# Second-layer loads on another queue, gathered rows ahead of weights, a last sum behind a branch, and one projection by groups of banks, in a two-layer hybrid trunk

## The reference

```python
for i in range(2):
    xn = rms_norm(h, norm_mix[i])
    pa, pb, pc, pg = split(xn @ w_in[i])
    ya = stick_breaking_attention(pa)              # branch A
    yb = rwkv7_time_mix(pb, xn, v_first, ...)      # branch B, a recurrence over time
    yc = swa_sink_attention(pc, rel_bias, sinks[i])# branch C
    ga, gb, gc = split(sigmoid(pg))
    h = h + (ga*(ya@w_proj_a[i]) + gb*(yb@w_proj_b[i]) + gc*(yc@w_proj_c[i])) @ w_out[i]
    hn = rms_norm(h, norm_ffn[i])
    h = h + (dense_swiglu(hn) if i == 0 else moe_swiglu(hn))   # 3584 hidden; 8 experts, top 2
return rms_norm(h, norm_final)[:, 16:]
```

## Time and profile before

| | |
|---|---|
| runs of the kernel | 2175.71, 2181.25, 2180.25 us; median 2180.25 |
| profiled execution: its time, its span | 2186.38 us, 2184.4 us |
| granted TensorE clock, mean | 0.983 of full speed |
| TensorE busy; weight loads | 2111.3 us (97%); 1831.0 us (84%) |
| VectorE, ScalarE busy | 1465.5 us (67%), 1233.0 us (56%) |
| loads | 481.36 MB read from HBM, 221 GB/s over the span |
| chain that ended last | TensorE 90%, VectorE 6%, ScalarE 3% |

### The profile page before, as it was taken

How to read it: one execution, slowest core, us unless ns; L and a number is a source line. 1 busy time by engine, 2 the same in 40 slices (tenths; PEclk the granted TensorE clock), 3 DMA queues, 4 the chain that set the end, 5 groups by cost and what they waited for, 6 DMA issues and landing times.

```text
span 2184.4 us, 36173 instructions
## 1 busy us (share of the span) xinstructions
PE 2111.3 (97%) x15316; PEld 1831.0 (84%) x15316; DVE 1465.5 (67%) x1329; ACT 1233.0 (56%) x1148; POOL 22.8 (1%) x24
## 2 busy tenths in 40 slices
PE   9999899999999999999998999999999999999997
PEld 7877689999999787788987888888888888888886
DVE  5633338554443764334847889898888889889894
ACT  4454345334332445445436777777777777777673
POOL 0000100000000000010000000000000000000000
PEclk9999899999999999999999999999999999999997
DMA  6332105434443232210635989899898999899892
GB/s 244 116 95 102 55 4 193 155 119 191 155 183 148 77 116 95 80 41 3 232 116 224 362 341 366 355 354 375 330 373 332 362 342 375 350 348 377 330 374 92
DMA packets 73839, 484.89 MB, mean 222 GB/s; under 512 B 12424, under 2 KB 13576, under 8 KB 15992
## 3 DMA queue, kind: packets, MB, share of 16 engines
q1 hardware_dynamic: 69960, 478.62, 56.6%
q10 hardware_dynamic: 3760, 4.52, 0.7%
HBM read 481.36 MB, written 1.74 MB: 221 GB/s over the span
## 4 chain that ended last, share of the span: by engine, by line
PE 90%; DVE 6%; ACT 3%; issue 1%; DMA 1%; ACTq 0%; DVEq 0%; SPq 0%
PE PS L510 23%; PE PS L512 22%; PE PS L511 22%; PE PS L906 5%; PE PS L772 2%; PE PS L790 2%; DVE area L1717 2%; DVE WL L1717 1%; PE PS L1154 1%; PE PS L1161 1%; PE PS L651 1%; PE PS L814 1%; ACT WH L1631 1%; PE PS L565 1%; PE PS L853 1%
## 5 line engine op out<-in xcount | busy, mean ns | idle before, releaser
L1717 DVE TENSOR_TENSOR WL<-ring,WH 128x2048 fp32r<-128x2048 f32 x410 | 934.5, 2289 | 266.4 <-ACT WH L1286 152.8
L1631 ACT ACTIVATE WH<-ring 128x2048 fp32r<-128x2048 f32 x336 | 643.0, 1916 | 170.8 <-PE PS L512 147.5
L510 PE MATMUL PS<-WH,XGH 128*128 128x512 f32 x896 | 355.0, 396 | 6.6 <-DVE XGL L1717 5.9
L512 PE MATMUL PS<-WL,XGH 128*128 128x512 f32 x896 | 350.7, 391 | 0.0
L511 PE MATMUL PS<-WH,XGL 128*128 128x512 f32 x896 | 350.1, 391 | 0.0
L1286 ACT ACTIVATE WH<-ring 128x2048 fp32r<-128x2048 f32 x74 | 141.4, 1911 | 130.0 <-PE PS L512 129.9
L510 PEld LDWEIGHTS PS<-WH,XGH 128*128 128x128 f32 x896 | 169.0, 189 | 41.6 <-DVE XGL L1717 6.1
L512 PE MATMUL PS<-XL,WH 128*128 128x272 f32 (+1 forms) x704 | 202.5, 288 | 0.0
L512 PEld LDWEIGHTS PS<-WL,XGH 128*128 128x128 f32 x896 | 168.7, 188 | 36.1
L511 PEld LDWEIGHTS PS<-WH,XGL 128*128 128x128 f32 x896 | 169.2, 189 | 33.6
L510 PE MATMUL PS<-WH,HTH 128*128 128x512 f32 x448 | 176.5, 394 | 0.6
(11 more groups left out here) (339 smaller groups left out, 3580.1 us busy)
## 6 DMA issues: line engine op xcount, KB each, us to landing
ring<-in_experts SPq DMA_DIRECT2D x336, 1024.0 KB, 6.7
ring<-in_weights SPq DMA_DIRECT2D x114, 1024.0 KB, 6.8
ring<-in_weights SPq DMA_DIRECT2D x4, 576.0 KB, 6.2
ring<-in_weights SPq DMA_DIRECT2D x4, 512.0 KB, 4.4
cst<-in_consts ACTq DMA_DIRECT2D x1, 1731.0 KB, 8.6
area<-in_x ACTq DMA_DIRECT2D x2, 512.0 KB, 4.9
out<-area SPq DMA_DIRECT2D x4, 256.0 KB, 2.2
bias_line<-lin SPq DMA_DIRECT2D x1, 672.0 KB
```

The source lines that it names most:

```text
L510: pe.matmul(o, lh, rh, start=first, stop=False, skip_group_check=True)
L512: return pe.matmul(o, lh, rl, start=False, stop=last, skip_group_check=True)
L1631: act.activation(WH[(BASE + j + 1) % 3][:, :], ring[b][:, 2048 * (j % 2):2048 * (j % 2) + 2048], ACT.Copy).then_inc(S("w_hi"), 1)
L1717: tt = lambda o, a_, b_, op: dve.tensor_tensor(o, a_, b_, op)
```

## The change

It has four parts. The seven loads for layer 1 move from ScalarE to SyncE, behind the load of the second chunk after the first branch's. `first_select` runs `gathered_low` before half chunks 1 and 2. The last expert's sum moves from the end of `expert_hidden` to a place behind the overflow branch (in the loop of the overflow it goes into `first_select`), the barrier there is replaced by waits on `fin_dve` and `fin_act`, and ScalarE's square starts after the first of the two additions. The last branch's projection runs by groups of four banks: for banks 0 to 3 all four row tiles, out of both half chunks, then the same for banks 4 to 7; its events on ScalarE and VectorE are hung earlier or in another order.

```diff
@@ SyncE
+            def second_layer_loads():
+                def load_later(d_, s_):
+                    sp.dma_start(d_, s_).then_inc(S("low_rank1"), 16)
+                low_rank(1, load_later)
+                load_later(vw1_sb[:, :, :], vw1[0].rearrange("(k p) n -> p k n", p=P))
+                load_later(vw2_sb[:, :], vw2[0])
+                load_later(router_sb[:, :, :], router[0].rearrange("(k p) n -> p k n", p=P))
             for i, (l, name, width) in enumerate(chunks):
+                if i == position[(0, f"P{MERGE_ORDER[0]}")] + RING:
+                    second_layer_loads()
@@ TensorE
+            def rows_by_banks(l, name, lo, xh, xl, before, mid):
+                g = split_half[(l, name)]
+                for group in range(2):
+                    for half in range(2):
+                        wh, wl = half_ready(g + half)
+                        if half == 0:
+                            before(4 * group)
+                        for d_ in range(4 * group, 4 * group + 4):
+                            for i in range(2):
+                                k, c = 2 * half + i, slice(i * D + d_ * P, i * D + d_ * P + P)
+                                ins = three_products(PS[:, d_, lo:T], wh[:, c], wl[:, c], xh(k), xl(k), k == 0, k == 3)
+                        if group:
+                            ins.then_inc(S("w_used"), 1)
+                    if group == 0:
+                        ins.then_inc(S(mid), 1)
...
+                    if j == 2:
+                        rows_by_banks(l, f"P{b}", lo, lambda k: YH[b][:, k, lo:], lambda k: y_lo[:, k, lo:],
+                                      lambda d_: pe.wait_ge(S("m_s"), at("m_s", l, 4 + d_ // 4)), "m_p")
+                        continue
...
             for_all_experts(pe, expert_products, first_gather)
-            end_stage(pe, "pe")
             for q in range(2):
-                column_sums([(4 * q, 4 * q + 4)], "fin_dve" if q else "fin_act", 1).then_inc(S("fin_pe"), 1)
-                pe.wait_ge(S("fin_dve" if q else "fin_act"), 2)
+                column_sums([(4 * q, 4 * q + 4)], "fin_dve" if q else "fin_act", 3 if q else 1).then_inc(S("fin_pe"), 1)
+                pe.wait_ge(S("fin_dve" if q else "fin_act"), 4 if q else 2)
@@ ScalarE
-                if l == 0:
-                    def load_later(d_, s_):
-                        act.dma_start(d_, s_).then_inc(S("low_rank1"), 16)
-                    low_rank(1, load_later)
...
                 for h in range(2):
-                    after_half(events, l, f"P{MERGE_ORDER[2]}", 1).append((merged_high, h))
+                    after_half(events, l, f"P{MERGE_ORDER[2]}", h).append((merged_high, h))
...
-            end_stage(act, "act")
+            act.wait_ge(S("fin_dve"), 1)
             act.activation(squares_of(DEPTH, 0)[:, 0:4, META:], hT[:, 0:4, META:], ACT.Square).then_inc(S("fin_act"), 1)
@@ VectorE
-                        after_half(events, l, f"P{b}", 1 if j else 0).append((gated, j, h))
+                        after_half(events, l, f"P{b}", j % 2).append((gated, j, h))
                         if j == 2:
-                            after_half(events, l, f"P{b}", 1).append((merged_low, h))
+                            after_half(events, l, f"P{b}", h).append((merged_low, h))
...
-                dve.wait_ge(S("e_sc"), n + 1)
-                halves = lambda x_: x_.rearrange("p (a b) n -> p a b n", b=2)
-                for i, b in enumerate((2, 6)):
-                    o = halves(hT[:, 4 * i:4 * i + 4, META:T])
-                    ins = tt(o, o, PS[:, b:b + 2, :].rearrange("p a (b n) -> p a b n", b=2), ALU.add)
-                link_e(4, ins)
+                if not last:
+                    dve.wait_ge(S("e_sc"), n + 1)
+                    add_expert(0)
+                    link_e(4, add_expert(1))
...
                 expert_low(run * NE, 0)
                 if isinstance(run, int) and run == 0:
                     gate_weights()
-                for j in range(1, 3):
+                gathered_low(run * (NE + 1) + 1)
+                for j in range(1, AHEAD):
                     expert_low(run * NE, j)
-                gathered_low(run * (NE + 1) + 1)
-                for j in range(3, AHEAD):
-                    expert_low(run * NE, j)
-
-            for_all_experts(dve, expert_hidden, first_select)
-            end_stage(dve, "dve")
+            for_all_experts(dve, expert_hidden, first_select, last_scattered)
+            dve.wait_ge(S("e_sc"), NE)
+            add_expert(0).then_inc(S("fin_dve"), 1)
+            add_expert(1).then_inc(S("fin_dve"), 1)
+            dve.wait_ge(S("fin_dve"), 2)
```

More of the change, by code:

```diff
@@ L417, in expert_loads, with for_all_experts @@
                     sp.dma_start(ring[b][:, 2048 * half:2048 * half + 2048], experts[e, 2 * i + half, :, :]).then_inc(S(f"landed{b}"), 16)
-        def for_all_experts(eng, body, before=None):
+        def for_all_experts(eng, body, before=None, after=None):
             if before:
@@ L434, in for_all_experts, with low_rank @@
                     body(eng, NE - 1, again * NE + (2 * NE - 1), again + 1, True)
+                if after:
+                    after(eng)
+        def low_rank(l, ld):
+            ld(wwa[0:64, :], w2[l])
+            ld(wwa[64:P, :], a2[l])
+            ld(wg0[:, :], g2[l, 0:P, :])
+            ld(wg1[:, :], g2[l, P:P + 32, :])
         def overflow_branch(eng):
@@ L1253, in _ @@
             load(relb[:, :], rel_bias)
-            def low_rank(l, ld):
-                ld(wwa[0:64, :], w2[l])
-                ld(wwa[64:P, :], a2[l])
-                ld(wg0[:, :], g2[l, 0:P, :])
-                ld(wg1[:, :], g2[l, P:P + 32, :])
             low_rank(0, load)
@@ L1499, in copied_output @@
                     act.activation(Y[:, :, c * CH:(c + 1) * CH], rows4(0), ACT.Copy).then_inc(S("r_yc"), 1)
-                if l == 0:
-                    def load_later(d_, s_):
-                        act.dma_start(d_, s_).then_inc(S("low_rank1"), 16)
-                    low_rank(1, load_later)
-                    load_later(vw1_sb[:, :, :], vw1[0].rearrange("(k p) n -> p k n", p=P))
-                    load_later(vw2_sb[:, :], vw2[0])
-                    load_later(router_sb[:, :, :], router[0].rearrange("(k p) n -> p k n", p=P))
                 g_first = first_split[l]
@@ L1691, in _ @@
             ins.then_inc(S("fin_act"), 1)
-            act.wait_ge(S("fin_dve"), 3)
+            act.wait_ge(S("fin_dve"), 5)
             act.activation(MR[:, 184:186], MR[:, 184:186], ACT.Sqrt).then_inc(S("fin_act"), 1)
-            act.wait_ge(S("fin_dve"), 4)
+            act.wait_ge(S("fin_dve"), 6)
             for q in range(2):
@@ L2182, in expert_low, with add_expert @@
                    WH[(BASE + j + 1) % 3][:, :].bitcast(F32), ALU.subtract).then_inc(S("w_lo"), 1)
+            def add_expert(i):
+                halves = lambda x_: x_.rearrange("p (a b) n -> p a b n", b=2)
+                o = halves(hT[:, 4 * i:4 * i + 4, META:T])
+                return tt(o, o, PS[:, (2, 6)[i]:(2, 6)[i] + 2, :].rearrange("p a (b n) -> p a b n", b=2), ALU.add)
             def expert_hidden(dve, e, n, run, last):
@@ L2265, in first_select @@
                 if not (isinstance(run, int) and run == 0):
+                    dve.wait_ge(S("e_sc"), run * NE)
+                    add_expert(0)
+                    v_e(run * (NE * 5), add_expert(1))
                     ins = dve.tensor_scalar(slots, slots, -float(SLOTS), None, ALU.add)
@@ L2274, in first_select, with last_scattered @@
                     gate_weights()
-                for j in range(1, 3):
+                gathered_low(run * (NE + 1) + 1)
+                for j in range(1, AHEAD):
                     expert_low(run * NE, j)
-                gathered_low(run * (NE + 1) + 1)
-                for j in range(3, AHEAD):
-                    expert_low(run * NE, j)
-            for_all_experts(dve, expert_hidden, first_select)
-            end_stage(dve, "dve")
+            def last_scattered(dve):
+                dve.wait_ge(S("e_sc"), PASSES * NE)
+            for_all_experts(dve, expert_hidden, first_select, last_scattered)
[3 more added lines that the diff above has]
+            dve.wait_ge(S("fin_dve"), 2)
             tt(squares_of(DEPTH, 0)[:, 4:8, META:], hT[:, 4:8, META:], hT[:, 4:8, META:], ALU.mult).then_inc(S("fin_dve"), 1)
@@ L2290, in _ @@
             dve.reciprocal(MR[:, 184:186], MR[:, 184:186]).then_inc(S("fin_dve"), 1)
-            dve.wait_ge(S("fin_dve"), 4)
+            dve.wait_ge(S("fin_dve"), 6)
             for q in range(2):
```

## The result

The changed kernel takes 2158.44 us, median of 4 runs (2156.52 to 2165.53), the kernel before in the same comparison 2180.75 us, median of 4. The ratio is 0.9903, with a 95% interval of 0.9874 to 0.9933: about 1% faster, 22.3 us between the medians. The forecast was 2155 with a range of 2150 to 2164. The profiled execution has a span of 2157.6 us and a time of 2159.41; before it was 2184.4 us of span.

The account below looks back on a forecast made before the run. TensorE, busy 97% of the span, was taken as the bound, with five stops to shorten. Gains of 5.3 + 9.9 + 5.0 + 5.2 = 25.4 us from the 2180.25 median gave 2155 us, range 2150 to 2164.

Parts of the forecast that it names:

- Loads: Start of layer 0's recurrence: without seven DMA issues ahead of ScalarE's first copy, 4.3 us plus 1.0 of clock, 5.3 us.
- VectorE's last two opening operations: Start of layer 0's recurrence: the last two of four operations opening the inverse take 1.3 us, ending at 246.25.
- The clock's part: Layer 0's recurrence: without the stop, 240 matmuls lose less time at half clock; 1.16 us counted, 1.0 taken.
- Banks: Output product after the last branch: no stop before its first half; gain 5.0 us in layer 0, 4.9 in layer 1.
- the tie: Layer 0's output product, second half: VectorE's low half and TensorE's first half product both end at 419.55; start put at 419.65.
- Rival 1: Output product: the stop moves to before the second half; if all the banks' gain goes, 2165 us. Chance 0.07.
- Gathered rows: First expert's first product: starts 3.55 us earlier, plus 1.5 of clock; 5.0 us, bounds 3.5 and 6.2.
- The clock's 1.5: First expert: of some 2.7 us lost at half clock after the stop, 1.5 gained; bounds 0 and 2.7.
- Rival 4: Expert stage becomes bound by its loads, one starting 2.1 us later; at 128 us an expert, 2186 us. Chance 0.02.
- Last sum: Final norm: VectorE's flag reading and branch hidden before the adds, so TensorE starts its sums earlier; gain 5.2 us.
- from there to the end nothing changes: Final norm, from TensorE's first column sums to the kernel's end: stays 14.3 us, at half clock.
- Rival 3: Final norm: the branch is not hidden, TensorE's being longer; sum loses 1.2 to 3.9, giving 2156 to 2159. Chance 0.05.

Follow-up runs that it names:

- the later mask: Changed kernel with GpSimd's first mask of each recurrence block waiting until VectorE has opened the inverse: 2156.49 us, ratio 0.9896.
- the part alone: Kernel before with only the gathered rows' low part moved ahead of the two weight half chunks; its time is not in the text given.
- fills: Changed kernel plus idle products of ones with a constant on TensorE, three ahead of the first gather and five behind it: 2153.37 us, ratio 0.9880.
- the six products ahead of the sums: Changed kernel plus six products of ones with a constant on TensorE between the branch and the first column sum: 2159.51 us, ratio 0.9930.
- the kernel with the fills at the end: Changed kernel with TensorE's branch ahead of the last scatter, five idle products before that scatter and five behind it: 2153.87 us, ratio 0.9889.

## Why the prediction was right, step by step

The sign, the range and the place of each gain were right; the sum was 25.4 us, and 22.3 came between the medians, 21.1 by the ratio. What I call measured is by place, in the table above. There the two profiled executions have 18.3 us between them, and the means over all executions 21.4; by these means no term is larger than its forecast, so part of how close the medians came is luck.

**Loads: 5.3 forecast, 3.6 measured** (3.3 alone; 4.5 to 4.8 against the kernels of this series that keep the loads). The mechanism was right: ScalarE's first copy comes 1.26 us after the stage's start (1.5 at most was named), and nothing behind SyncE's issues was late. The term mis-sized is VectorE's last two opening operations. I took 1.3 us for both, which is what layer 1 of the trace before has (0.43 and 0.84); in layer 0 they took 0.98 and 1.37, as GpSimd's masks ran beside them. The trace of the kernel before had this already, 0.95 and 1.37 in the same place. The sum should have been read from there. That the later mask brings TensorE's next product to 3.69 us after the start, where the sum had 3.9, shows it. The 240 products behind took 8.67 us, not 8.27. The clock's part was sound: it fell to half 6.0 to 7.5 us behind the stage's start in all four kernels with the loads on ScalarE, and in none of the nine others.

**Banks: 5.0 and 4.9 forecast, 4.7 and 4.7 measured.** No stop ahead of the first half; ahead of the second 0.15 us in layer 0, where the tie was put at 0.1, and 0.36 in layer 1, a little over the 0.3 that was named as the most. By the steps VectorE needed 6.1 us behind the branch's end; it took 6.02 (402.36 to 408.38). Rival 1 did not come about, and the clock stayed at full in both places, as assumed, in all nine kernels with this part.

**Gathered rows: 5.0 forecast, 1.8 to 7.0 measured** (3.5 between the means). The stop went from 5.88 to 2.44 us, 3.44 of the 3.55 forecast; the first product comes 2.4 us after the gather's end (2.3 was named). The clock's 1.5 was sized as if there were one outcome, and there are two. In some executions the clock is at half during the gather and again behind it, in others (among them the part alone) not at all; first gather to second is then 119.7 to 121.9 or 116.7 us. Without this part it is not one figure either, 121.5 to 123.65, and the profile before, from which I read the loss, has the largest. On the mean the clock gave nothing back. Which outcome comes went by where the clock had fallen before the gather; that fills hold it rests on one execution and on the time of that kernel. Rival 4's mechanism was seen, at a small size: in one execution of the changed kernel TensorE waited for the first expert's weights, 1.2 us in two waits; in the five kernels above that have this order too, from the part alone to the six products ahead of the sums, no such wait appears, and the experts kept to 124.1 us.

**Last sum: 5.2 forecast, 3.5 measured** (3.9 alone). VectorE's standstill is hidden as assumed, its adds start 0.2 us after the scatter's end, and the first column sum comes 4.72 us after the scatter's start, where 5.06 was forecast. The step that failed is "from there to the end nothing changes": the end took 16.3 us instead of 14.3. Rival 3 had TensorE's branch as the danger and looked at the wrong end of it. The branch ended 0.4 us before the square was ready; what was exposed is the 2.37 us standstill two products behind it. In the kernel before, 5.9 us lay between branch and sums, which covers the 3.0 to 3.6 us after which TensorE went on elsewhere. The Trainium skill ("Advanced Engine Details and Errata", Control Flow Timing) gives some 0.1 us for a compare-and-branch; the rows here have 0.05 to 0.06 us on ScalarE and VectorE and 3.36 to 3.90 on TensorE, and the standstill comes on top.

**The clock** gave something that can be counted on at the recurrence and at the banks, where the stops are gone, and nothing of the kind at the gather and the end, where stops of 1.6 to 2.6 us are left. The 7.6 us by which the changed kernel's profile was early at layer 0's recurrence came by chance, and are most of why the two spans differ by more than the medians.

**Open:** when a stop comes behind TensorE's branch. Four of the five executions with the branch between the last scatter and the sums had one, and none of the eight others had, among them the one without a branch; and each stop ends 1.2 to 1.4 us after a packet of instructions has landed. That makes late instructions the cause as far as times can show it. No run moved the packets and nothing else. My simple form of it, that the stop comes along wherever the branch goes, is refuted by the run with the branch ahead of the scatter. In the kernel with the fills at the end the branch took 3.77 us, stuck out by 0.58 us, and ten records right behind it ran without a stop.

## What to carry to other kernels

Price an operation from a row with the same neighbours: four VectorE operations took 3.19 us where GpSimd worked beside them and 1.68 where it did not. A branch costs more than its own row, so put it where its engine has some microseconds of queued work or of waiting ahead of the next product, and read the engine's records and the packets of instructions behind it too. Where a stop cannot be removed, a few idle products in it may hold the clock, as in one execution at the gather and two at the end; six right behind the branch, with the clock already at half, only took 5.6 us. Before a clock term is priced, look at more than one execution: the same place gave 116.7 and 121.9 us.

## What the runs showed of the hardware

- TensorE's branch takes 3.36 to 3.90 us, and two or three products later TensorE may stand for 0.9 to 2.4 us more (four of five executions).
- Within that branch a packet of 16 KB of instructions lands, 1.46 to 1.55 us before the branch's end (twelve kernels); the stop behind it ends 1.25 to 1.44 us after the next such packet has landed.
- Four operations of VectorE on 128 x 256 take 3.19 us with GpSimd's masks beside them and 1.68 us without. Each slowed one ends 0.28 us after the mask that began before it (twelve in the changed kernel). GpSimd's masks take 0.73 and 1.27 us either way; in the kernel before, where the first began 0.01 us after an operation of VectorE, 1.01 and 1.44.
- While TensorE ran column sums (one column) and transposes (128 columns), busy for 6.20 of 7.00 us, the granted clock was 0.50, right behind a stretch at 1.00.
- With the same products of TensorE ahead, layer 0's recurrence started between 234.3 and 242.4 us, by where the clock happened to fall.
